# Differential attention scores: two fp32 products per step replaced by four single-pass f32r products, operands placed by GpSimd transfers

## What is computed

```
h = rms_norm_2(x, norm_pre[l])
u = h @ w_in[l]                      # a_q, a_k, a_v, a_z, b_..., c_..., g
def block(i):                        # 128 queries against all keys
    s = jnp.einsum('bqhmd,bkhmd->bhmqk', qb, kf) * scale      # m = 0, 1; d = 64
    s = jnp.where(rel >= 0, s + bias[None, :, None], NEG)
    pm = jax.nn.softmax(s, axis=-1)
    w = pm[:, :, 0] - lam * pm[:, :, 1]
    return jnp.einsum('bhqk,bkhe->bqhe', w, v)
```

## Time and profile before

| | |
|---|---|
| median of 3 runs | 2491.24 us (2490.59 to 2492.32) |
| profiled execution, first to last instruction (span) | 2486.4 us |
| median less span (start and end) | 4.8 us |
| PE busy | 2467.6 us, 99% of the span |
| DVE, ACT busy | 60%, 45% |
| POOL busy | 25.9 us |
| TensorE clock granted | 1.000 mean |
| differential attention, first and last score record | layer 0: 1288.9 to 1382, layer 1: 1907.1 to 2000 us |

### The profile page before, as it was taken

One profiled execution on the slowest core, in us unless ns is written; L12 is line 12 of the kernel. 1 busy time (PEld: TensorE's weight loads), 2 busy tenths in 40 slices (PEclk: granted clock), 3 DMA queues, 4 the chain that ended last, 5 costly groups with the idle time before them and its releaser, 6 DMA issues.

```text
span 2486.4 us, 32337 instructions
## 1 busy us (share of the span) xinstructions
PE 2467.6 (99%) x11940; PEld 1961.0 (79%) x11940; DVE 1486.3 (60%) x2518; ACT 1125.7 (45%) x2012; POOL 25.9 (1%) x18
## 2 busy tenths in 40 slices
PE   9999999999999999999999999999999999999999
PEld 7887888888776788888887777778877777777887
DVE  7987656566769753433456655664465665466435
ACT  6675433433546543442445543442354554444234
POOL 0000000000000000000000000000020000000002
PEclk9999999999999999999999999999999999999999
DMA  7633466666221123222221211222223121122233
GB/s 305 217 105 134 167 203 206 206 204 205 85 85 69 64 89 103 101 95 95 101 102 69 77 63 70 77 81 93 102 85 110 62 75 68 64 83 77 93 109 111
DMA packets 77902, 280.34 MB, mean 113 GB/s; under 512 B 8640, under 2 KB 8896, under 8 KB 77504
## 3 DMA queue, kind: packets, MB, share of 16 engines
q1 hardware_dynamic: 61056, 219.60, 25.1%
q10 hardware_dynamic: 16704, 58.79, 7.1%
HBM read 276.26 MB, written 2.10 MB: 112 GB/s over the span
## 4 chain that ended last, share of the span: by engine, by line
PE 92%; DVE 4%; ACT 2%; DMA 1%; issue 0%; SPq 0%; ACTq 0%
PE ps L222 26%; PE ps L224 25%; PE ps L223 25%; PE ps L1817 2%; PE ps L1914 2%; DVE wl L217 1%; PE ps L1887 1%; PE ps L1719 1%; PE ps L1157 1%; PE ps L1821 1%; PE ps L1219 1%; ACT wh L214 1%; PE ps L1776 1%; PE ps L1194 1%; PE ps L408 1%; PE ps L1992 1%
## 5 line engine op out<-in xcount | busy, mean ns | idle before, releaser
L217 DVE TENSOR_TENSOR wl<-raw,wh 128x1024 fp32r<-128x1024 f32 x372 | 456.7, 1228 | 592.0 <-ACT wh L214 592.0
L222 PE MATMUL ps<-xh,wl 128*128 128x512 f32 x1744 | 696.1, 399 | 3.8 <-DVE wl L217 2.4
L224 PE MATMUL ps<-xh,wh 128*128 128x512 f32 x1744 | 680.3, 390 | 0.0
L223 PE MATMUL ps<-xl,wh 128*128 128x512 f32 x1744 | 679.7, 390 | 0.0
L214 ACT ACTIVATE wh<-raw 128x1024 fp32r<-128x1024 f32 x372 | 392.8, 1056 | 600.7 <-PE ps L224 589.7
L222 PE MATMUL ps<-bh,wl 128*128 128x512 f32 x1174 | 463.3, 395 | 2.7 <-DVE crow L1181 1.5
L224 PE MATMUL ps<-bh,wh 128*128 128x512 f32 x1174 | 457.3, 390 | 0.0
L223 PE MATMUL ps<-bl,wh 128*128 128x512 f32 x1174 | 457.2, 389 | 0.0
L222 PEld LDWEIGHTS ps<-xh,wl 128*128 128x128 f32 x1744 | 327.1, 188 | 122.4 <-issue 37.6
L224 PEld LDWEIGHTS ps<-xh,wh 128*128 128x128 f32 x1744 | 327.3, 188 | 69.9
L223 PEld LDWEIGHTS ps<-xl,wh 128*128 128x128 f32 x1744 | 327.6, 188 | 65.5 <-issue 1.2
(11 more groups left out here) (322 smaller groups left out, 2543.4 us busy)
## 6 DMA issues: line engine op xcount, KB each, us to landing
raw<-in_w SPq DMA_DIRECT2D x388, 512.0 KB, 3.2
bA<-in_ada ACTq DMA_DIRECT2D x74, 512.0 KB, 4.5
bC<-in_ada SPq DMA_DIRECT2D x9, 512.0 KB, 12.0
bD<-in_ada ACTq DMA_DIRECT2D x8, 512.0 KB, 4.6
bS<-in_attn_bias ACTq DMA_DIRECT2D x8, 512.0 KB, 3.2
bD<-in_ada SPq DMA_DIRECT2D x7, 512.0 KB, 14.3
bC<-in_ada ACTq DMA_DIRECT2D x6, 512.0 KB, 4.3
h<-in_x SPq DMA_DIRECT2D x4, 512.0 KB, 7.7
```

The costliest lines, as they stand in the source:

```text
L217: e.tensor_tensor(wl[p][:], raw[p][:], wh[p][:].bitcast(F32), ALU.subtract)\
L222: e.matmul(out, wl[p][:, blk, 0:M], xhi, start=start, stop=False)
L223: e.matmul(out, wh[p][:, blk, 0:M], xlo, start=False, stop=False)
L224: return e.matmul(out, wh[p][:, blk, 0:M], xhi, start=False, stop=stop)
```

## The change

Each head's query and key is split like a weight: ACT writes the rounded upper part (hi), DVE the rest (lo), both f32r, into slots 8 and 9 of `bh` and `bl`. GpSimd transfers then place them so that a product uses all 128 rows. For map m the stationary tile holds the query's hi in rows 0 to 63 and its lo in rows 64 to 127 (4 transfers a head). For the moving side there are two tiles, the key's hi in both halves and the key's lo in both halves (8 transfers a head). One product with the first and one with the second add up to (hi + lo) x (hi + lo). The tiles of two heads alternate. A new semaphore `s_qk` counts the transfers; PE waits for all twelve of a head ahead of its first score (`parts_ready`).

`combine(k)`, which stood before the scores of step k+1, now follows the exponentials of its own step. `plan` becomes 1, 1, 2, 2.

```
+        s_qk = sem("s_qk")
...
+                if it.kind == "head":
+                    hi, lo = bh[:, 8 + it.k, :], bl[:, 8 + it.k, :]
+                    if act:
+                        done(e.activation(hi, src, ACT.Copy), it.name + "hi")
+                    if dve:
+                        need(it.name + "hi")
+                        done(e.tensor_tensor(lo, src, hi.bitcast(F32), ALU.subtract), it.name + "lo")
+                        need(it.name + "lo")
+                        e.sem_inc(s_bank[bank], 1)
...
                 if act or not low_later:
                     split(it.u + 2, 0, 0)
+                if it.kind == "head" and pool:
+                    if it.wait:
+                        it.wait()
+                    need(it.name + "hi")
+                    need(it.name + "lo")
+                    for x, m, to in it.dst:
+                        src = (bh, bl)[x][HD * m:HD * m + HD, 8 + it.k, :]
+                        e.dma_start(to, src).then_inc(s_qk, 16)
...
-                            r = slice(HD * m, HD * m + HD)
-                            done(e.matmul(ps[2 + m][:, 0:nk(n)], q(n // NT)[r, P * i:P * i + P], k(n // NT)[r, 0:nk(n)],
-                                          start=True, stop=True), f"{s}{n}sc{m}")
+                            x, (kh, kl) = q(n // NT)[m][:, P * i:P * i + P], k(n // NT)
+                            e.matmul(ps[2 + m][:, 0:nk(n)], x, kh[m][:, 0:nk(n)], start=True, stop=False)
+                            done(e.matmul(ps[2 + m][:, 0:nk(n)], x, kl[m][:, 0:nk(n)], start=False, stop=True), f"{s}{n}sc{m}")
...
-                dq, dk = (lambda t: bC[:, t % 2, :]), (lambda t: bC[:, 2 + t % 2, :])
+                lower, upper = slice(0, HD), slice(HD, P)
+                def dq(t):
+                    return [bh[:, 4 * (t % 2) + m, :] for m in range(2)]
+                def dk(t):
+                    return [[x[:, 4 * (t % 2) + 2 + m, :] for m in range(2)] for x in (bh, bl)]
+                def query_parts(t):
+                    return [(x, m, dq(t)[m][(lower, upper)[x], :]) for m in range(2) for x in range(2)]
+                def key_parts(t):
+                    return [(x, m, dk(t)[x][m][r, :]) for x in range(2) for m in range(2) for r in (lower, upper)]
+                def parts_ready(t):
+                    e.wait_ge(s_qk, 16 * (12 * NT * l + 12 * (t + 1)))
...
-                plan = [2, 2, 1, 1] * 3 + [2, 2, 2, 2] + [0, 0, 0]
+                plan = [1, 1, 2, 2] * 3 + [2, 2, 2, 2] + [0, 0, 0]
...
-                    if 0 <= k < N:
-                        combine(k)
...
                         if pe and (k + 1) % NT == 0:
-                            for it in heads[(k + 1) // NT]:
-                                out_of(it)
+                            parts_ready((k + 1) // NT)
                         scores(k + 1)
                         maximum(k + 1)
                     outs = fill(halves, plan[k + 1], state)
                     if k + 1 < N:
                         exponentials(k + 1)
+                        combine(k + 1)
```

More of the change, by code:

```diff
@@ L2066, in scored, with run @@
                 def scored(t):
-                    return (lambda: need(f"{s}{4 * t - 5}sc1")) if t > 1 else None
-                heads = [[Unit("copy", f"{n}aq{t}", dq(t), scored(t), ready=n + "n" if t == 0 else None), Unit("copy", f"{n}ak{t}", dk(t), scored(t))] for t in range(4)]
+                    def run():
+                        if t > 1:
+                            need(f"{s}{4 * t - 5}sc1")
+                        parts_ready(t - 1)
+                    return run if t else None
+                heads = [[Unit("head", f"{n}aq{t}", query_parts(t), scored(t), ready=n + "n" if t == 0 else None),
+                          Unit("head", f"{n}ak{t}", key_parts(t), k=1)] for t in range(4)]
                 silu = [Unit("silu", f"{n}az{t}", bS[:, t, :]) for t in range(4)]
```

## The result

| | before | after |
|---|---|---|
| median of 4 runs each | 2490.91 us (2490.48 to 2492.32) | 2518.84 us (2516.26 to 2519.98) |
| span of the profiled execution | 2486.4 us | 2516.2 us |
| granted clock, mean | 1.000 | 0.992 |

The changed kernel takes 1.0111 times as long (95% interval 1.0099 to 1.0122), 27.9 us more. The 4.8 us that I had put around a span are 1.8: the profiled execution of the changed kernel took 2517.98 us at a span of 2516.2, and the other executions of both kernels show the same 1.8. The profiled execution of before was therefore about 3 us faster than the median. The forecast adds a difference to the median, so nothing in it rests on this.

The account below looks back on a forecast made before the run. PE was taken as the bound, busy 99% of the span and 92% of the last chain. Terms: -10.4 (matmuls) + 26.8 (transfer stalls) + 5.4 (clock) = +21.8 us on 2491.2, so 2513 us; range 2480 to 2530.

Parts of the forecast that it names:

- The matmuls: PE's scores and return to the projection: 4.11 us a head become 2.86; with 0.4 a layer, 10.4 us gained.
- the way back to the projection: First projection matmul behind each step's scores takes 0.43 us instead of 0.23: 0.80 us a head before the change.
- Splitting: ACT's copy replaced by one of equal size, 16 DVE subtractions of 0.69 us hidden behind PE's next unit: costs nothing.
- The earlier combination and the plan: Half units behind the 384-key step remove a wait inside the 512-key scores, counted as part of their 1.42 us.
- The transfers: GpSimd's eight key transfers land in 9.0 us; PE stalls 5.0 us in head 0, 2.8 in others: 26.8 us.
- seven issues plus one flight: Landing of the key's last transfer: 7 x 0.91 us of issue distance plus 2.6 us from issue to landing, 9.0 us.
- The floor: 1024 KB in one transfer lands in 5.6 us, so even free issues leave head 0 waiting 1.6 us a layer.
- the case that movement sets the pace: If movement, not issue, sets the pace, head 0 waits only 1.6 us a layer; quick case changes under 1 us.
- the signs that I gave for being wrong: GpSimd's issues closer than 0.62 us, or the last transfer landing well off 2.6 us behind its issue.
- that turning point: GpSimd issue distance of 0.62 us, at which, without the clock, the stalls reach the 10.4 us gain.
- the quick rival: GpSimd issues 0.45 us apart, landing after 5.75 us, stalls 3.5 us in two layers: 2484 us; quick transfers' chance 0.36.
- The clock: PE's clock falls behind head 0's two 5.0 us stalls, 2.7 us each, not behind those of 2.8: 5.4 us.

Follow-up runs that it names:

- order alone: The kernel before with the combination behind its own step's exponentials and the plan 1, 1, 2, 2; fp32 scores, no GpSimd transfers: 2487.90 us.
- no transfers: The changed kernel without GpSimd's transfers and the wait for them; hi and lo written straight into one tile each, scores not the reference's: 2479.41 us.
- the filled waits: The changed kernel with unused matmuls ahead of each wait for the parts, 20 for head 0 and 9 for the others: 2507.07 us.
- the plan of before: The changed kernel with the half units of the projection again 2, 2, 1, 1; the early combination stays: 2507.35 us.
- half the transfers: The changed kernel with only parts that change partitions transferred, 2 for the query and 4 for the key a head: 2481.33 us.

## Why the prediction was right, step by step

**The matmuls (forecast 10.4 us, waits inside the scores included).** The records of the changed kernel:

```profile
1323.06 0.27 PE L1738 MATMUL ps<-bl,bh 128*128 128x128 f32 x1
1323.17 0.27 PE L1737 MATMUL ps<-bh 128*128 128x128 f32 x1
...
1366.33 0.39 PE L1738 MATMUL ps<-bl,bh 128*128 128x512 f32 x1
1366.56 0.39 PE L1737 MATMUL ps<-bh 128*128 128x512 f32 x1
```

0.11 us apart with 128 keys and 0.23 with 512 (256 keys: 0.12, 384 keys: 0.17), as estimated. The gain was nevertheless 12.7, and it doesn't come from where I looked for it. The wait inside the 512-key scores, which I counted as part of 1.42, is worth 2.7 to 3.0 of it. The other 10.0 come mostly from a price of the 64-row fp32 scores that I did not see: they start late behind the values. Before, and without transfers:

```profile
1341.87 0.83 PE L1776 MATMUL ps<-bT,bD 128*128 128x128 f32 x6
1342.63 0.70 PE L1719 MATMUL ps<-bC 64*128 64x256 f32 x4
```

```profile
1313.37 0.83 PE L1786 MATMUL ps<-bT,bD 128*128 128x128 f32 x6
1313.95 0.36 PE L1729 MATMUL ps<-bh 128*128 128x256 f32 x1
```

From the values to the scores it is 0.76 us before and 0.58 now. The other three steps of the head differ by the same 0.18, so 32 steps make 5.8 us. The starts in the two timelines (order alone and no transfers, the four steps of one head) give the rest: from the first score record to the projection 2.94 against 2.83 us a head, and from the first projection matmul to the second 1.37 against 0.99. Over eight heads the score products themselves thus gain 0.9 us and the way back to the projection 3.0, 3.9 together, for which my sum had 10.4 less the 3.0, 7.4. The 0.43 us of the first projection matmul overstated the way back: it starts 0.33 to 0.36 us ahead of the next one. That 10.4 lies near 10.0 and 12.7 is luck.

**Splitting (nothing).** Held: there is no new wait of PE for ACT or DVE in the list, and without transfers the full gain arrives.

**The earlier combination and the plan.** I gave the removal of the wait to the half units. It is the combination's. The plan costs 10 us where the transfers have to be covered. The cover itself was near: in head 1, 5.7 us from the first issue (1314.54) to the start of the wait (1320.24), forecast 6.2. What I had not done is to price the plan as a loss of cover.

**The transfers (distance 0.91, flight 2.6, landing 9.0 us; stalls 26.8).** Here two errors cancel. Issues are 0.50 us apart and not 0.91; the flight of the last is 4.8 us and not 2.6. Landing 8.4 instead of 9.0, first issue half a microsecond later than I had it, so the stalls are 25.8: 4.82 and 4.97 for head 0 (forecast 5.0), 2.2 to 3.1 for the others (2.8). The step that failed is "seven issues plus one flight" with the flight of a lone small transfer. The floor that I put beside it, 1024 KB in 5.6 us, at least says that bytes count, but it was 2.7 us short of the 8.3 that the same bytes took here, and with it I set aside the case that movement sets the pace. Both of the signs that I gave for being wrong came true: the issues are closer than 0.62 us, and the last landing lies 4.8 us behind its issue. By that turning point the measured distance would have meant "faster"; the quick rival failed by its flight, not by its distance. With the 4.8 us in its place: 7 x 0.50 + 4.8 = 8.3.

**The clock (5.4 us, two stalls only).** Too small by half: 10.5 us by the filled waits. Behind the 4.8 us stall of head 0 twelve matmuls at 0.43 cost 12 x 0.20 = 2.4, near the 2.7 that I took. What was wrong is the exemption of the shorter stalls: behind 2.65 us the clock is 0.58 for 4 us, behind 2.19 us 0.68. An estimate from the windows above, each length times what its clock lacks to 1.00, gives 3.1 and 1.7 us behind head 0 of the two layers and 6.6 behind four of the other six, 11.4 in all. The earlier trace rows showed one idle stretch of 4.4 us, and from it nothing follows on shorter ones.

The sum by what was measured: -12.7 + 25.8 = 13.1, and 12.2 us to the 25.3 of the stages, of which 10.5 came back with the filled waits. 1.7 us stay unassigned, or 0.8 with the estimate of 11.4. To the 27.9 us of the medians 2.6 are missing; runs of the changed kernel alone lie 3.7 us apart.

The forecast that this is slower, and by PE's waits for the key's parts, was right for the reason given. That the number was right within 6 us is luck in part: the issue distance was 0.41 us too long seven times over (2.9 us a landing) and the flight 2.2 us too short, while the gain of the matmuls was 2.3 us too small and the cost of the clock 5.1 us.

Open: why the last transfer of head 1 took 6.1 us with the plan of before, and behind which of the waits of 2.2 to 2.9 us the clock falls. No run took the weights out, so their share in a flight rests on the two windows of the kernel with half the transfers.

## What to carry to other kernels

Count what must land, in bytes, and not only in issues: eight 128 KB transfers behind each other took 8.4 us to the first score and four took 4.9. Halving what is moved turned a loss of 28 us into a gain of 10. When an operand must be placed on other partitions, write what already stands right in place and move only the rest.

A wait of PE can cost more than its length where PE is the bound: 25.8 us of waits cost 10.5 more through the clock. Where a wait can't be removed, useless matmuls in it give that part back.

## What the hardware showed that I had not expected

- GpSimd issues transfers of 64 partitions by 2 KB 0.50 us apart, about as fast as SP's queue (0.45). About 0.5 us lie between the end of DVE's subtraction and the first issue.
- The same 128 KB transfer lands in 2.4 us (median with 6 a head), 4.7 (median of the key's lo parts with 12 a head) or 6.5 (the last of 12 in a row, in one head). The Trainium skill (DMA: Bandwidth & Descriptors, Anatomy of one DMA — SWDGE (gpsimd) path) gives a fit of 2.0 us plus the bytes over 436 GB/s, which makes 2.3 us for this size by estimate; the rows agree with 6 a head (2.4) and not with 12 (4.7).
- Declaring the transfer as fp32 leaves its time as it is (4.7 and 4.7 us), though it has fewer packets (4608 for 7680).
- PE without matmuls for 2.65 us was followed by 4 us at a mean granted clock of 0.58, for 2.46 and 2.89 us in other heads by a clock of 1.00, and of two waits of 2.33 us in one kernel one was followed by 0.57 and the other by 1.00.
- 64-row fp32 scores behind 128-row fp32 values start 0.18 us later than 128-row f32r scores do.
